# A decoder trunk on one core: the second output-projection block as split products, and two ring blocks exchanged

## The reference

```python
ada = silu(c) @ W_ada[l] + b_ada[l]          # shift1, scale1, gate1, shift2, scale2, gate2
...
merged = g_att * y_att + g_conv * y_conv + g_rwkv * y_rwkv
x = x + (1.0 + gt1[:, None, :]) * (merged @ w_out[l])
h = modulate(rms_norm(x, norm2_g[l]), sh2, sc2)
x = x + (1.0 + gt2[:, None, :]) * peer_ffn(h, peer_w_q[l], ...)   # begins with q = h @ w_q
...
return rms_norm(x, final_g)
```

## Time and profile before

| what | value |
|---|---|
| median of three runs | 2843.02 us (2840.32 to 2843.39) |
| the profiled execution | 2842.12 us |
| its span, first to last instruction | 2840.3 us |
| TensorE busy | 2746.5 us (97%) |
| VectorE busy | 2239.8 us (79%) |
| ScalarE busy | 1158.6 us (41%) |
| GpSimd busy | 568.2 us (20%) |

### The profile page before, as it was taken

One profiled execution on the slowest core, in us unless ns is written; L12 is line 12 of the kernel. 1 busy time (PEld: TensorE's weight loads), 2 busy tenths in 40 slices (PEclk: granted clock), 3 DMA queues, 4 the chain that ended last, 5 costly groups with the idle time before them and its releaser, 6 DMA issues.

```text
span 2840.3 us, 51143 instructions
## 1 busy us (share of the span) xinstructions
PE 2746.5 (97%) x19786; PEld 2492.1 (88%) x19786; DVE 2239.8 (79%) x4318; ACT 1158.6 (41%) x1664; POOL 568.2 (20%) x354
## 2 busy tenths in 40 slices
PE   6999999999999999999999999999999999999998
PEld 6998887899999997877899988788999999977776
DVE  7998676578977658888879987766889666688887
ACT  4533421244444444333355343222444444433334
POOL 0000002120876730000000000030227776000000
PEclk9999999999999999999999999999999999999998
DMA  7553351465888778888745434344468877788885
GB/s 295 184 187 119 146 201 29 162 229 195 220 233 240 202 226 295 280 281 286 244 151 190 178 112 190 122 140 154 180 209 221 239 232 192 264 283 288 285 287 187
DMA packets 258985, 593.81 MB, mean 209 GB/s; under 512 B 82608, under 2 KB 198064, under 8 KB 200240
## 3 DMA queue, kind: packets, MB, share of 16 engines
q1 hardware_dynamic: 192656, 572.74, 57.9%
q0 software_dynamic: 36864, 0.15, 2.6%
q10 hardware_dynamic: 29216, 17.57, 2.1%
HBM read 537.27 MB, written 53.08 MB: 208 GB/s over the span
## 4 chain that ended last, share of the span: by engine, by line
PE 79%; DVE 11%; DMA 5%; ACT 3%; issue 2%; POOL 0%; SPq 0%; DVEq 0%; ACTq 0%; POOLq 0%
PE ps L1197 25%; PE ps L1176 17%; PE ps L687 13%; PE ps L649 6%; DMA act_rows<-region 4%; PE ps L1186 2%; DVE u_lo L2113 2%; PE ps L777 2%; PE ps L1062 2%; PE ps L727 2%; PE ps L939 1%; DMA ring<-in_stream 1%; DVE region L1721 1%; PE ps L1009 1%; PE ps L996 1%
## 5 line engine op out<-in xcount | busy, mean ns | idle before, releaser
L1176 PE MATMUL ps<-h_hi,u_hi 128*128 128x256 f32 x2048 | 589.0, 288 | 11.7 <-DVE u_lo L2113 11.1
L1176 PE MATMUL ps<-h_lo,u_hi 128*128 128x256 f32 x2048 | 579.2, 283 | 0.0
L1176 PE MATMUL ps<-h_hi,u_lo 128*128 128x256 f32 x2048 | 579.0, 283 | 0.0
L2360 POOL DMA_INDIRECT gate_rows<-route x256 | 476.4, 1861 | 297.3 <-DVE route L2227 134.0
L2113 DVE TENSOR_TENSOR u_lo<-ring,u_hi 128x1024 fp32r<-128x1024 f32 x256 | 312.5, 1221 | 205.8 <-ACT u_hi L1513 205.6
L1176 PEld LDWEIGHTS ps<-h_hi,u_hi 128*128 128x128 f32 x2048 | 392.3, 192 | 18.2 <-DVE u_lo L2113 17.6
L1176 PEld LDWEIGHTS ps<-h_lo,u_hi 128*128 128x128 f32 x2048 | 392.7, 192 | 0.0
L1176 PEld LDWEIGHTS ps<-h_hi,u_lo 128*128 128x128 f32 x2048 | 392.3, 192 | 0.0
L1534 ACT ACTIVATE u_hi<-ring 128x1024 fp32r<-128x1024 f32 x192 | 203.9, 1062 | 323.8 <-PE ps L1197 323.8
L2120 DVE TENSOR_TENSOR u_lo<-ring,u_hi 128x1024 fp32r<-128x1024 f32 x192 | 234.9, 1223 | 51.5 <-ACT u_hi L1534 51.2
L1541 ACT ACTIVATE region<-ps 128x256 f32<-128x256 f32 x256 | 97.9, 383 | 423.2 <-PE ps L1176 256.7
(11 more groups left out here) (394 smaller groups left out, 5196.8 us busy)
## 6 DMA issues: line engine op xcount, KB each, us to landing
ring<-in_stream SPq DMA_DIRECT2D x456, 1024.0 KB, 5.4
act_rows<-region SPq DMA_DIRECT2D x256, 128.0 KB, 5.5
gate_rows<-rstd ACTq DMA_DIRECT2D x2, 8192.0 KB, 29.7
region<-gate_rows SPq DMA_DIRECT2D x256, 64.0 KB, 4.0
region<-act_rows SPq DMA_DIRECT2D x128, 128.0 KB, 4.5
small_inverse<-act_rows SPq DMA_DIRECT2D x128, 128.0 KB, 4.3
gate_rows<-route POOLq DMA_INDIRECT x256
region<-in_c SPq DMA_DIRECT2D x7, 512.0 KB, 5.6
```

Of the source, the lines that this page charges most:

```text
L1176: ins = mm(ps[:, c % 4, 0:T], x, y[:, k, :], start=k == 0 and i == 0, stop=k == KD - 1 and i == 2)
L2360: gp.indirect_dma_start(gate_cells, bass.IndirectOffsetOnAxis(ap=gate_at[:, r:r + 1].bitcast(I32), axis=0), gate_weight[:, r:r + 1], None, ...
```

## The change

`W_OUT[1]` becomes a split block as well: ScalarE makes its high part into `ow_hi[0]`, VectorE its rest, and `m_lo` is made before the loop. `W_OUT[2]` takes `ow_hi[1]`, and `W_OUT[3]` takes `ow_hi[0]` again, for which ScalarE waits until `W_OUT[1]` has been added (`x_added` of 2). In the stream `W_OUT[2]` and modulation block 10 change places: block 70 is now modulation block 10, block 71 is `W_OUT[2]`. On VectorE modulation block 9 moves from behind the first to behind the second addition, and modulation block 10 behind the rest of `W_OUT[3]`, in front of the third addition. The count at which the query blocks begin goes up by one.

```diff
@@ -49,8 +49,8 @@
 LATE_GATE = MIX_O + 4 * N_O + 1
 OUT = LATE_GATE + GATES_LATE
 RWKV_O = tuple(OUT + i for i in range(N_O))
-W_OUT = tuple(OUT + N_O + 2 * i for i in range(N_O))
-ADA_LATE = tuple(n + 1 for n in ATT_O[:3] + CONV_O[:1]) + tuple(n + (2 if n == CONV_O[0] else 1) for n in CONV_O + W_OUT)
+W_OUT = OUT + 4, OUT + 6, OUT + 9, OUT + 10
+ADA_LATE = tuple(n + 1 for n in ATT_O[:3] + CONV_O[:1]) + tuple(n + (2 if n == CONV_O[0] else 1) for n in CONV_O) + (OUT + 5, OUT + 7, OUT + 8, OUT + 11)
 W_Q = OUT + 3 * N_O
 PEER = W_Q + H * 2 * P // T
 CHUNKS = KEYS
@@ -421,8 +421,8 @@
             i = n - Z_GATE if n < MIX_O else N_GATE - GATES_LATE + n - LATE_GATE
             return gates[:, 2 * i:2 * i + 2, :]
 
-        split_at = {MIX_O - 2: Z_GATE - Z + 1, MIX_O - 1: Z_GATE - Z + 2, W_OUT[2]: Z_GATE - Z + 4, W_OUT[3]: Z_GATE - Z + 5}
-        merged_at, query_at = Z_GATE - Z + 3, Z_GATE - Z + 6
+        split_at = {MIX_O - 2: Z_GATE - Z + 1, MIX_O - 1: Z_GATE - Z + 2, W_OUT[1]: Z_GATE - Z + 4, W_OUT[2]: Z_GATE - Z + 5, W_OUT[3]: Z_GATE - Z + 6}
+        merged_at, query_at = Z_GATE - Z + 3, Z_GATE - Z + 7
 
         def own_half(b):
 
@@ -1142,10 +1142,10 @@
                     for n in RWKV_O:
                         rwkv_part(n, (2 * g, 2 * g + 1))
                 project(W_OUT[0], merged, ready=S["merged_ready"])
-                project(W_OUT[1], merged)
-                split_block(W_OUT[2], ow_hi[0], m_hi, m_lo, merged_at)
+                split_block(W_OUT[1], ow_hi[0], m_hi, m_lo, merged_at)
+                split_block(W_OUT[2], ow_hi[1], m_hi, m_lo, merged_at)
                 norm_sum(1, 0, 4)
-                split_block(W_OUT[3], ow_hi[1], m_hi, m_lo, merged_at)
+                split_block(W_OUT[3], ow_hi[0], m_hi, m_lo, merged_at)
                 norm_sum(1, 4, KD)
                 def key_scores(h):
 
@@ -1483,10 +1483,13 @@
                 root_table()
                 act.wait_ge(S["merged_ready"], 4)
                 A(m_hi[:, :, :], merged, ACT.Copy).then_inc(S["zw_hi"], 1)
+                part_hi(W_OUT[1], ow_hi[0])
                 for i, n in enumerate(W_OUT):
-                    if i in (1, 2):
-                        part_hi(W_OUT[i + 1], ow_hi[i - 1])
+                    if i == 0:
+                        part_hi(W_OUT[2], ow_hi[1])
                     act.wait_ge(S["x_added"], i + 1)
+                    if i == 1:
+                        part_hi(W_OUT[3], ow_hi[0])
                     square(2 * i)
                     was_read(act, n)
                     square(2 * i + 1)
@@ -2079,19 +2082,23 @@
                     vec.tensor_tensor(merged[:, 2 * i:2 * i + 2, :], merged[:, 2 * i:2 * i + 2, :], t, ALU.add).then_inc(S["merged_ready"], 1)
                 dve.wait_ge(S["c_silu"], 2)
                 late_ada(8)
+                dve.wait_ge(S["zw_hi"], merged_at)
+                vec.tensor_tensor(m_lo[:, :, :], merged, m_hi[:, :, :].bitcast(F32), ALU.subtract).then_inc(S["zw_lo"], 1)
+                part_lo(W_OUT[1], ow_hi[0])
                 for i, n in enumerate(W_OUT):
-                    if i == 1:
-                        dve.wait_ge(S["zw_hi"], merged_at)
-                        vec.tensor_tensor(m_lo[:, :, :], merged, m_hi[:, :, :].bitcast(F32), ALU.subtract).then_inc(S["zw_lo"], 1)
                     dve.wait_ge(used, taken(n))
                     for a in range(2):
                         k = 2 * i + a
                         vec.scalar_tensor_tensor(xT[:, k, :], pair(n)[:, a, :], gate1[:, 0, k:k + 1], xT[:, k, :], ALU.mult, ALU.add)\
                             .then_inc(bank_read[bank(n)] if a else S["x_added"], 1)
-                    if i in (1, 2):
-                        part_lo(W_OUT[i + 1], ow_hi[i - 1])
-                    if i < 3:
-                        late_ada(9 + i)
+                    if i == 0:
+                        part_lo(W_OUT[2], ow_hi[1])
+                    if i == 1:
+                        late_ada(9)
+                        part_lo(W_OUT[3], ow_hi[0])
+                        late_ada(10)
+                    if i == 2:
+                        late_ada(11)
                 def query_lo(h):
 
                     n = W_Q + h
```

## The result

The changed kernel takes 2862.43 us in the median (2859.68 to 2865.46, 4 runs) against 2842.81 us of the kernel before, a ratio of 1.0073 with a 95% interval of 1.0059 to 1.0087: 19.6 us slower. One execution of the kernel before, in the series of e0, e9, e10 and e11, took 8480.63 us in the slow state and is left out of the ratios. The direction was forecast; the time lies 12.4 us above the forecast and outside its range. The profiled execution took 2863.95 us, 21.8 us more than the profiled one of before.

What follows compares the result with a forecast made beforehand. The bound was taken as a chain of waits through TensorE's products and the ring's loads. Landing 2.45 plus clock 1.3 us a layer, twice 7.5 us, on the profiled 2842.12 or the median 0.9 above gave 2850.0 us; range 2846 to 2853.5.

Steps and rivals of the forecast that it cites:

- the path: Waits setting the last w_out addition: first block, 71's load, high part, third block's product at about 584.2 us.
- the second block's gain: Second w_out block as split products: TensorE work shrinks 1.17 us, ending at 580.7 instead of 581.5, buying nothing.
- the landing term: Third w_out block, now 71, lands later behind 70, delaying the last addition 2.45 us a layer.
- VectorE's queue behind the late high part: VectorE waits about 5.7 us before the third block's rest, then reaches the last addition at 597.8, tied with TensorE.
- the half clock: After TensorE's 3.5 us gap before the third block, 1.2 GHz costs 1.3 us a layer, bounds nothing to 1.7.
- The late first query block: Rival: block 74's load, behind two modulation blocks, comes late, at most 1.6 us a layer more, 2851 to 2853; chance 0.10.
- a gap with dense work at both ends would mostly leave the clock alone: Rival: clock stays up behind TensorE's gap before the third block, so 4.9 us in all, 2847.9 us; chance 0.25.
- the sum: Landing 2.45 plus clock 1.3 make 3.75 us a layer, twice 7.5 us, giving 2850.0 us.
- The landing of block 71: Block 71, issued behind 70, takes 6.8 us and lands at 582.1 instead of 579.65, 2.45 us later.
- Everything behind it shifted by the same amount, with no slack to take it up, as the queries start only from the norm.: Behind the last w_out addition, the same shift was to be found again at the end of the layer.

Runs made afterwards that it cites:

- e0: The kernel before run again, nothing altered, for a second profile: 2842.86 us, ratio 0.9997.
- e9: The kernel before plus 64 one-column product records a layer between norm sums and first query block, results unused: 2858.59 us, ratio 1.0058.
- e10: The kernel before plus 128 one-column product records a layer between norm sums and first query block, results unused: 2891.20 us, ratio 1.0168.
- e11: The changed kernel with w_out and modulation blocks reordered and ScalarE squaring the second block before the last block's high part: 2853.11 us, ratio 1.0030.
- e2: The kernel before with only blocks 70 and 71 exchanged, second w_out block still plain: 2851.23 us, ratio 1.0036.
- e7: The changed kernel run again, nothing altered, giving the second series and second profile: 2858.27 us, ratio 1.0056.
- e6: The kernel before plus 16 one-column product records a layer between norm sums and first query block, results unused: 2847.22 us, ratio 1.0014.
- e12: The changed kernel with blocks reordered, second and third w_out blocks split and the last plain, so no more records than before: 2841.55 us, ratio 1.0000.
- e1: The changed kernel with blocks 70 and 71 back in their old places: 2850.24 us, ratio 1.0034.
- e5: The kernel before plus 45 extra products a layer between the last w_out block and the last norm sums, results unused: 2856.34 us, ratio 1.0054.
- e4: The changed kernel plus 32 extra products in TensorE's gap before the third w_out block, results unused: 2852.70 us, ratio 1.0037.

## Why the prediction was wrong

Right were the path (first block, load of 71 behind 70, high part, third block), that the second block's gain is of no use (it did not even appear: the block ended at 581.75, before at 581.5), the size of the landing term where nothing else falls on it (2.45, e2: 2.5), and VectorE's queue behind the late high part (6.75 us of waiting, forecast 5.7). Right in kind was the half clock: 1.3 us taken, 7.47 - 5.98 = 1.5 measured in the first layer and 7.97 - 5.99 = 2.0 in the second, over the bound of 1.7. The late first query block did not come about. By the Trainium skill ("TensorE: Matmul & The Clock Gate", "Part 1: The HAM clock gate") the clock goes down after at least one idle window; my reading of it, that a gap with dense work at both ends would mostly leave the clock alone, did not come true. Behind the gaps of 4.0, 4.4, 4.3 and 4.3 us (changed kernel and e7, both layers) it fell, behind the 2.55 and 2.53 us of e2 it did not; this fits the page's rule as it stands, but does not test it.

Two steps failed. The stretches cost 10.6 us instead of the 7.5 of the sum, 3 of the 12.4 us by which the forecast was missed. The larger part, 9.0 us (5.3 in the second series), arose behind them, where the sum had nothing.

*The landing of block 71*, "lands at 582.1 instead of 579.65, 2.45 us later". I took 6.8 us from the earlier trace rows as a property of the second load of a pair. It was 8.1 and 7.6 us in the first profile, 8.1 and 8.2 in the second. So 0.8 to 1.4 us a layer are missing here, and a fetch of TensorE's instructions falls into this transfer each time; in the kernel before it fell into block 69, whose 8.7 us were not on the chain. e2, without a fetch on that load, has 6.67 us. The warning stood in my own rows: the 7.5 us of block 75 in the earlier trace rows belong to a load with a fetch in it. Why the fetch comes later here is not shown. In the first layer it comes 11.6 us after the start of the first block instead of 6.8, in the second 7.9 instead of 6.5, so that a stream consumed faster cannot be the reason. With this term the stretch comes to 2.45 + 1.3 + 1.5 = 5.3 us in the first layer and 2.45 + 0.8 + 2.0 = 5.3 in the second, which is what was measured.

*"Everything behind it shifted by the same amount, with no slack to take it up, as the queries start only from the norm."* This named slack as the only possible surprise. The queries lost 2 us more to a second stretch of half clock, and the first 40 activations of PEER 8.5 us in the first profile, 5.3 in the second (6.1 and 1.5 over all 128). e6 shows that 16 more product records a layer can lengthen PEER alone, e9 and e10 that 64 and 128 do not, and e12 that the split block without more records does not. The size agrees: 2.9 us a layer, 5.8 a kernel, stand beside the 5.6 us that e1 has beyond its stretches and the 4.8 of e6. What is shown is that the number of records, and with it the position of TensorE's stream, decides; that the packets of queue 8 are the means is argued, from their count and from the period of 128 that e10 bears out, and stays open. The count of records stood in the earlier trace rows (x32 and x48), and I used it only as a time.

Open remains how PEER's loss builds up: that a delayed store passes its delay round the ring of ScalarE, VectorE, SyncE and DMA is my guess, which I have not followed turn by turn. Also open are the 4 us of e2 beyond its stretches, nearly as much as the 16 records cost in e6. The kernel before scatters from 2836 to 2850 us over all series, and its second profile has a stretch of 28.6 us in one layer, where block 70 took 5.70 us to land instead of 4.85; I have not looked for the cause. Each "first 40" stands on one profile.

## What to carry to other kernels

When a load is moved in a queue that is served strictly in order, read the landing time of the place it is moved to, not that of the place it leaves: a slot that is free early is worth nothing behind a load whose slot is not. Where a stretch is paced by DMA round trips, an edit that changes the number of instructions shifts the instruction fetches of everything behind it, and can cost time far from its own place; a control with the same number of instructions and no other change (e6) tells this from the edit's own effect. Judge a gain of 1 us in such a kernel against several such shifts, not against one baseline.

## What the runs showed of the hardware

- The load of block 71 (1 MB, issued half a microsecond behind another) landed after 6.7 to 6.8 us in the six layers of before, e2 and e5, where no instruction packet fell into it, and after 7.6 to 8.2 us in the eight layers of changed, e7, e1 and e4, where one packet of 16 KB did.
- Queue 8 moved 160 packets of 16 KB for 19818 products and as many weight loads, one for some 124 (changed kernel).
- 128 one-column products took 0.203 us each in e10; the granted clock fell to 0.50 behind the first 1.3 us and stood there to their end, 26 us after the start. 32 and 45 products of 256 columns (e4, e5) ran at 0.120 us each with the clock at 1.00.
- Gaps of 4.0 and 4.4 us in TensorE's dense work brought 3.4 and 6.8 us at 1.2 GHz (changed kernel), of 4.3 us in both layers of e7 3.4; those of 2.55 and 2.53 us brought none (e2).
